# A fourth pair's q and k through the front's seven-product rounds, and P times V one tile a step

## The chip, the cores and the metric

One Trainium2 chip, and of it one core. The metric is the time of one execution on the device, in microseconds (us), by the median of several runs; the lower, the better.

## The reference

One layer of an encoder on x of 1024 rows (the sequence) by 1024 columns, in float32.

```python
h = rms_norm(x, g_pre_mix)
hc, bg, cg, q, k, v = jnp.split(h @ w_in, 6, axis=-1)          # six times 512 columns
y_conv = short_gated_conv(hc, bg, cg, w_conv)                  # bg * causal_conv3(cg * hc)
y_attn = chunked_band_attention(q, k, v, rel_bias)             # 8 heads of 64
y = jnp.concatenate([group_rms_norm(y_conv, g_conv_out, 8),
                     group_rms_norm(y_attn, g_attn_out, 8)], axis=-1) @ w_out
x = x + rms_norm(y, g_post_mix)
gate, up = jnp.split(rms_norm(x, g_pre_ffn) @ w_ffn_in, 2, axis=-1)
x = x + rms_norm((silu(gate) * up) @ w_ffn_out, g_post_ffn)    # 2816 hidden columns
```

In the attention a chunk of 64 queries sees its own chunk and the 8 before it: scores of q and k over 8, a learned bias by relative position, softmax, times v.

## The kernel before

Every engine has a hand-written program, and semaphores join them. Each float32 matrix product is made of three matmuls in fp32r: an operand is split into a high part (ScalarE) and a low part (VectorE), and high by high, high by low, low by high are summed in PSUM.

**The front.** Of the input projection, v is made first. Then come `FRONT` rounds of two 128-column chunks of `w_in` each. A round multiplies two by two blocks with seven block products in place of eight (`front_multiply`, L1171, twelve matmuls of 512 columns for a product). VectorE makes the sums of weights (`front_s`), the low parts (`front_low`) and the sums of products (`make_u2` to `make_c12`). Five rounds make the convolution's three inputs but for two chunks. The other `FRONT_PAIRS` rounds make q and k of one head pair each, the last pair first. All but the last round's q and k are stored in `query_scratch` (`store_qk`) and loaded again (`load_qk`) when the front's rows of the arena come free; pair 0's go directly into its operands. The loads of v and then of q, k are issued on SP's queue (L616, L653) once product 5 of the last round is done.

**The chunks that fill.** What the front does not make is made by `project`: `FILLED` chunks, 48 matmuls of 512 columns each, cut into eight pieces of six matmuls (`piece`, L934). They are the convolution's gate `cg` of the last group first and `bg` of it last, and between them q and k of the pairs that the front leaves out. `AHEAD` pieces run before attention. The table `FILLS` says how many run in each step of each pair. A finished half is drained from PSUM by ScalarE (q, k) or multiplied by VectorE (`cg`, `bg`).

**The attention.** Four head pairs `t`, each with nine steps `s`. A tile is 128 queries of both heads; tile `i` sees at most 640 keys (tiles 0 to 3 see 128 to 512). The parts of a tile:

- scores (L948), one PSUM area for each head; tiles 0 and 1 are scored together in step 0, tiles 2 and 3 in step 2, tiles 4 to 7 in their own steps. Scores of a tile wait for the biases of the one before (`biased`), since its area is the same.
- bias and row maximum on VectorE (`add_bias`, L2242), one instruction for each head and a small accumulator read behind it
- exponential on ScalarE (L1603)
- in the next step, transposes of P on TensorE (`transpose_p`, L958), four blocks for each head copied by ScalarE (`read_pT`, L1612) and, from tile 4 on, a fifth block (L966) copied by VectorE (`read_pT`, L2250)
- P times V (`times_v`, L976). Its result stands with head columns on the partitions, so it is copied by VectorE (`copy_o`, L2256), two tiles in one copy, transposed back by TensorE (`turn_back`, L984) and read by VectorE (`read_o`, L2261).

After a pair, ScalarE squares the outputs, VectorE sums the squares (L2366), GpSimd makes the factors (L773) and VectorE scales (`o_scale`, L2376). TensorE transposes the result (`transpose_o`, L1067), and VectorE multiplies it by the gain (`o_finish`, L2385). These four lie in steps 1 to 3 of the next pair. VectorE also makes the low parts of the next pair's q and k in step 7 (`low_q`, L2280, `low_k`, L2284) and, spread over the steps by `TAP_STEPS`, the last convolution's three taps.

Each engine takes its work strictly in the order written in its `step(t, s)`; nothing reorders it.

The out projection (L1219), the feed-forward products (L1334) and the last products (L1361) follow.

## Time and profile before

| | us |
|---|---|
| median of 3 runs | 1093.37 |
| lowest, highest | 1093.21, 1093.54 |
| the profiled execution | 1093.39 |
| its span | 1091.6 |
| TensorE busy | 1082.3 |
| VectorE busy | 795.6 |
| ScalarE busy | 473.5 |
| GpSimd busy | 150.9 |

The span is from the first to the last instruction on the core; the execution's own time has 1.8 us more around it. A row of a timeline has the start, the busy time, engine, line, operation, what it writes and reads, the shape and the number of instructions merged. Since TensorE's matmuls overlap in the pipeline, the time that a group takes from TensorE is read from its start to the start of the next row; the busy time in the row is some 0.1 us more. In brackets stands the idle time of the engine before the row, and what ended it.

The attention stretch runs from the first scores of pair 0 at 222.17 us to the end of pair 3's last transposes at 351.53.

### The profile page before, as it was taken

Reading aid. Unit: us, or ns where it says so; the run is one execution under the profiler, and the core shown is the slowest. Engines: PE = TensorE matmul, PEld = TensorE weight load, DVE = VectorE, ACT = ScalarE, POOL = GpSimd, SP = SyncE. Lnnn points to the kernel's source line nnn. Section 1 sums busy time; section 2 is a strip of 40 time slices with the busy share of each in tenths; the row PEclk is TensorE's granted clock in tenths of the full one; section 3 lists DMA queues with packets and bytes.
Section 4 is the critical chain, followed back from the end, with each engine's and each line's share of the span. In section 5 each row is a group of like instructions: output and inputs, shape, how many; then the busy total and the mean of one; then the engine's idle time right before and its main releaser. Section 6 shows DMA issues by size and latency. Waiting matters only on the chain.

```text
span 1091.6 us, 15835 instructions
## 1 busy us (share of the span) xinstructions
PE 1082.3 (99%) x5549; PEld 897.8 (82%) x5549; DVE 795.6 (73%) x1247; ACT 473.5 (43%) x802; POOL 150.9 (14%) x255
## 2 busy tenths in 40 slices
PE   8999999999999999999999999999999999999997
PEld 7888888878888888888888888888888888888886
DVE  6878888656767876968777878777787786555584
ACT  6642243356667665643232323323232256444541
POOL 2400000001101122102211211221121110000030
PEclk9999999999999999999999999999999999999999
DMA  7332123470010643517435543743554689777631
GB/s 270 107 126 77 43 58 127 160 251 2 21 59 20 231 158 114 172 50 249 139 118 188 173 154 116 221 140 119 183 175 151 210 322 363 232 232 231 212 115 77
DMA packets 117333, 168.28 MB, mean 154 GB/s; under 512 B 7880, under 2 KB 73432, under 8 KB 117280
## 3 DMA queue, kind: packets, MB, share of 16 engines
q1 hardware_dynamic: 99648, 107.50, 30.5%
q0 software_dynamic: 16464, 55.89, 14.7%
q10 hardware_dynamic: 1168, 4.20, 1.0%
q8 instruction: 32, 0.52, 0.2%
q14 instruction: 21, 0.17, 0.0%
HBM read 121.65 MB, written 49.04 MB: 156 GB/s over the span
## 4 chain that ended last, share of the span: by engine, by line
PE 95%; DVE 3%; DMA 1%; ACT 1%; issue 0%; POOL 0%; SPq 0%; DVEq 0%; POOLq 0%; ACTq 0%
PE psum L1334 35%; PE psum L1361 19%; PE psum L1171 11%; PE psum L934 8%; PE psum L1219 8%; PE psum L1083 4%; PE psum L976 3%; PE psum L948 2%; PE psum L958 2%; PE psum L923 1%; DMA arena<-in_x 1%; PE psum L1067 0%; PE psum L984 0%; PE psum L966 0%; PE psum L1180 0%
## 5 line engine op out<-in xcount | busy, mean ns | idle before, releaser
L1334 PE MATMUL psum<-arena_r,ws 128*128 128x512 f32 x960 | 224.1, 389 | 0.0
L1334 PEld LDWEIGHTS psum<-arena_r,ws 128*128 128x128 f32 x960 | 180.2, 188 | 37.4
L1334 PE MATMUL psum<-hT,ws 128*128 128x512 f32 x720 | 169.9, 389 | 0.0
L1334 PEld LDWEIGHTS psum<-hT,ws 128*128 128x128 f32 x720 | 135.1, 188 | 28.0
L1361 PE MATMUL psum<-hT 128*128 128x512 f32 (+1 forms) x600 | 135.2, 385 | 0.0
L1361 PEld LDWEIGHTS psum<-hT 128*128 128x128 f32 x600 | 111.3, 188 | 22.5
L2536 DVE TENSOR_TENSOR misc<-misc,psum 128x512 f32<-128x512 f32 x100 | 68.5, 685 | 48.3 <-PE psum L1334 46.1
L934 PE MATMUL psum<-hT,ws 128*128 128x512 f32 (+1 forms) x432 | 95.9, 373 | 0.0
L1171 PE MATMUL psum<-arena_r,ws 128*128 128x512 f32 x372 | 86.9, 389 | 0.0
L1814 ACT ACTIVATE ws<-o_raw 128x512 fp32r<-128x512 f32 x40 | 25.1, 628 | 138.5 <-DVE o_raw L2514 138.0
L934 PEld LDWEIGHTS psum<-hT,ws 128*128 128x128 f32 x432 | 72.5, 189 | 13.9 <-issue 2.2
L1171 PEld LDWEIGHTS psum<-arena_r,ws 128*128 128x128 f32 x372 | 69.8, 188 | 14.5
L1219 PE MATMUL psum<-ws,hT 128*128 128x512 f32 x348 | 81.2, 392 | 0.0
L1361 PE MATMUL psum<-ws 128*128 128x512 f32 (+1 forms) x348 | 78.1, 382 | 0.0
L1219 PEld LDWEIGHTS psum<-ws,hT 128*128 128x128 f32 x348 | 64.7, 188 | 13.3
L1361 PEld LDWEIGHTS psum<-ws 128*128 128x128 f32 x348 | 63.8, 188 | 12.6
L1171 PE MATMUL psum<-hT,ws 128*128 128x512 f32 x288 | 68.1, 390 | 0.0
L1814 ACT ACTIVATE ws<-raw 128x512 fp32r<-128x512 f32 x80 | 49.7, 623 | 40.3 <-PE psum L1334 39.3
L1171 PEld LDWEIGHTS psum<-hT,ws 128*128 128x128 f32 x288 | 53.9, 188 | 11.8 <-DVE ws L2044 0.7
L2531 DVE TENSOR_TENSOR ws<-raw,ws 128x512 fp32r<-128x512 f32 x80 | 55.2, 691 | 6.6
L2610 DVE TENSOR_TENSOR hT<-arena,hT 128x512 fp32r<-128x512 f32 x62 | 40.1, 688 | 20.0 <-ACT hT L1861 19.6
L1411 ACT ACTIVATE misc<-arena 128x1024 bf16<-128x1024 f32 (+2 forms) x37 | 34.8, 941 | 39.8 <-DVE arena L2662 16.6
(272 smaller groups left out, 1566.3 us busy)
## 6 DMA issues: line engine op xcount, KB each, us to landing
raw<-in_w_ffn_in SPq DMA_DIRECT2D x44, 512.0 KB, 4.4
act_scratch<-arena POOLq DMA_DIRECT2D x77, 256.0 KB, 3.2
raw<-in_w_in SPq DMA_DIRECT2D x22, 512.0 KB, 4.1
arena<-in_w_ffn_out POOLq DMA_DIRECT2D x22, 512.0 KB, 5.7
arena<-act_scratch SPq DMA_DIRECT2D x38, 256.0 KB, 3.5
arena<-in_x SPq DMA_DIRECT2D x16, 512.0 KB, 6.2
raw<-in_w_out SPq DMA_DIRECT2D x16, 512.0 KB, 3.4
raw<-act_scratch SPq DMA_DIRECT2D x26, 256.0 KB, 3.3
```

Source lines behind the costliest of these rows:

```text
L934: last = mm(PP[pair][:, at:end] if to is None else to, w[wp], hT[:, hp, k, at:end], start=(k == 0 and (wp, hp) == (0, 0)), stop=(k == KT - ...
L976: last = mm(PP[3][h * HD:(h + 1) * HD, at:at + P], v_tile(first + j, t * P + h * HD, HD), pT_of(t, tile_i)[:, h, j * P:(j + 1) * P], start ...
L1083: last = mm(v_bank(i), hT[:, hp, k, i * P:(i + 1) * P], v_weights(wp, k), start=(k == 0 and part == 0), stop=k == 7 and part == (1 if i < ...
L1171: last = mm(blocks(front_bank(n, i)), w[:, k * P:(k + 1) * P], b_operand(i, part, k), start=fresh_bank and k == 0 and w is hi and part == ...
L1219: last = mm(pair[:, half * 512:(half + 1) * 512], a, ws[:, slot, wp, half * 512:(half + 1) * 512], start=(first is not None and a is hi an ...
L1334: last = mm(blocks(bank), w[:, k * P:(k + 1) * P], b_operand(i, part, k), start=fresh_bank and k == 0 and w is hi and part == 0, stop=k == ...
L1361: last = mm(bank[:, at:end], a[:, n * P:(n + 1) * P], b[:, at:end], start=fresh_bank and a is ah and b is bh, stop=i == NP - 1 and a is al ...
L1411: go(dst, src, ACT.Square, scale=scale, accum_out=acc).then_inc(done[0], 1)
L1814: go(w_op(i)[0], w_raw[i], ACT.Copy).then_inc(w_hi, 1)
L2531: tt(lo, w_raw[i], hi.bitcast(F32), ALU.subtract).then_inc(w_split, 1)
L2536: tt(out, a, bank, ALU.add).then_inc(made, 1)
L2610: tt(lo, raw_ring[c % RING][:, part * 512:(part + 1) * 512], hi.bitcast(F32), ALU.subtract).then_inc(out_split, 1)
```

## The change

`FRONT_PAIRS` is 4: there are nine front rounds, and `FILLED` becomes 2, so that only `cg` and `bg` of the last group are left as filling chunks. 16 pieces stand in place of 32; `AHEAD` is 4 as before, and 12 run inside attention in place of 28. The splits of two chunks on ScalarE and VectorE go, and q and k of pair 3 are stored and loaded as those of pairs 1 and 2 are.

P times V is made one tile in each step, of the tile three steps back (V1 in step 4, V2 in step 5); tiles 6 and 7 go into steps 0 and 1 of the next pair. The turning back stays in pairs of tiles, one step later than before (steps 4, 6, 8, and step 1 of the next pair). VectorE copies an output pair behind the biases of steps 4, 6, 8 and reads it in the same step. In steps 4 and 6 a piece stands behind the turning back.

The transposes of a finished pair's outputs go from the banks beside the scores (`psum[:, 2560:3584]`) into the upper halves of the first four banks' pairs, which hold scores; they stand in step 1, ahead of the scores of tiles 2 and 3, and wait for the biases of tiles 0 and 1. Scores of tile 3 wait for VectorE's read of them, which is now two instructions of 512 columns.

What moves, at three places. TensorE, pair 0, from the scores of tile 4 (L948, one line later in the changed kernel) to those of tile 5, before and then changed:

```order
L948 MATMUL psum<-ws 128x384 [waits biased]
L948 MATMUL psum<-ws 128x384 x5
L948 MATMUL psum<-ws 128x256 x6
L958 MATMUL psum<-ident,arena 128x128 [waits pT_act,exp_done]
L958 MATMUL psum<-ident,arena 128x128 x7
L934 MATMUL psum<-hT,ws 128x512 [waits half_free1,w_split]
L934 MATMUL psum<-hT,ws 128x512 x5
L948 MATMUL psum<-ws 128x384 [waits biased]
```

```order
L949 MATMUL psum<-ws 128x384 [waits biased]
L949 MATMUL psum<-ws 128x384 x5
L949 MATMUL psum<-ws 128x256 x6
L974 MATMUL psum<-arena 64x128 [waits pT_act]
L974 MATMUL psum<-arena 64x128 x3
L959 MATMUL psum<-ident,arena 128x128 [waits pT_act,exp_done]
L959 MATMUL psum<-ident,arena 128x128 x7
L982 MATMUL psum<-ident,arena 128x128 [waits o_copied]
L982 MATMUL psum<-ident,arena 128x128
L935 MATMUL psum<-hT,ws 128x512 x6
L949 MATMUL psum<-ws 128x384 [waits biased]
```

Between the scores there stand now V1 and a turning back that waits for `o_copied`; the piece (L935) is behind it, where it followed T3.

TensorE, pair 0, from V4 in step 7 to T7 in step 8, before and then changed (L976 and L974 are P times V, L966 and L965 the fifth blocks):

```order
L976 MATMUL psum<-misc,arena 64x128 [waits tile_free,pT_dve,pT_act]
L976 MATMUL psum<-misc,arena 64x128 x9
L976 MATMUL psum<-arena 64x128 x10
L958 MATMUL psum<-ident,misc 128x128 [waits pT_act,exp_done]
L958 MATMUL psum<-ident,misc 128x128 x7
L984 MATMUL psum<-ident,arena 128x128 [waits o_copied]
L984 MATMUL psum<-ident,arena 128x128
L966 MATMUL psum<-ident,misc 128x128 x2
L934 MATMUL psum<-hT,ws 128x512 x6
L958 MATMUL psum<-ident,arena 128x128 [waits pT_act,exp_done]
```

```order
L974 MATMUL psum<-misc,arena 64x128 [waits pT_dve,tile_free,pT_act]
L974 MATMUL psum<-misc,arena 64x128 x9
L959 MATMUL psum<-ident,misc 128x128 [waits pT_act,exp_done]
L959 MATMUL psum<-ident,misc 128x128 x7
L965 MATMUL psum<-ident,misc 128x128 x2
L974 MATMUL psum<-arena 64x128 [waits pT_dve,pT_act]
L974 MATMUL psum<-arena 64x128 x9
L935 MATMUL psum<-hT,ws 128x512 x6
L959 MATMUL psum<-ident,arena 128x128 [waits pT_act,exp_done]
```

V5 left the side of V4, went behind T6 and got waits of its own (`pT_dve`); the turning back of step 7 went to step 8, and the piece stands behind V5.

VectorE, pair 1, steps 3 and 4, from behind the biases of tile 3, before and then changed:

```order
L2256 COPY arena<-psum 128x256 [waits o_psum]
L2085 TENSOR_SCALAR arena<-arena,params 128x1024
L2376 TENSOR_TENSOR arena<-o_raw,rst 128x1024 [waits o_rs,dve_seq]
L2240 MEMSET gate 128x1 [waits biased,scores_psum,o_ready]
L2242 ISA misc,nmax<-psum,arena 128x640
L2242 ISA nmax 128x1
L2240 MEMSET gate 128x1 [waits biased,scores_psum]
L2242 ISA misc,nmax<-psum,arena 128x640
L2242 ISA nmax 128x1
L2261 COPY o_raw<-psum 128x256 [waits o_back]
```

```order
L2373 TENSOR_TENSOR arena<-o_raw,rst 128x1024 [waits o_rs]
L2240 MEMSET gate 128x1 [waits biased,scores_psum,o_ready]
L2242 ISA misc,nmax<-psum,arena 128x640
L2242 ISA nmax 128x1
L2240 MEMSET gate 128x1 [waits biased,scores_psum]
L2242 ISA misc,nmax<-psum,arena 128x640
L2242 ISA nmax 128x1
L2256 COPY arena<-psum 128x256 [waits o_psum]
L2261 COPY o_raw<-psum 128x256 [waits o_back]
```

The copy of outputs 0 and 1 (waits `o_psum`) and the read after their turning back (`o_back`) both stand behind the biases of tile 4 now, and a tap left the place ahead of the scaling (waits `o_rs`). In step 3 of all pairs nothing else moved ahead of the scaling but the product with a gate half in pair 2.

The diff, cut to its core:

```diff
-    FRONT_PAIRS = 3
+    FRONT_PAIRS = 4
...
-        FILLS = [[1, 1, 1, 1, 1, 0, 1, 0, 1], [1, 1, 1, 1, 1, 0, 1, 0, 1], [1, 1, 1, 1, 1, 0, 1, 0, 1], [1, 2, 1, 1, 1, 0, 1, 0, 0]]
-        TAP_STEPS = (9, 11, 20)
+        FILLS = [[1, 0, 0, 1, 1, 0, 0, 0, 1], [0, 0, 0, 1, 1, 0, 0, 0, 1], [0, 0, 0, 1, 1, 0, 0, 0, 1], [0, 0, 0, 1, 1, 0, 0, 0, 0]]
+        TAP_STEPS = (5, 6, 10)
...
+        FILL_LAST = (4, 6)
...
-        OT_BANKS = psum[:, 2560:3584]
+        OT_BANKS = psum[:, 0:2048].rearrange("p (b h c) -> p h b c", h=2, c=512)[:, 1]
...
-                if i in (2, 4, 6):
-                    turn_back(t, i - 2)
-                elif n > 4:
-                    pe.wait_ge(tile_free, tile(t, i - 1) + 1)
+                if i in (3, 5, 7):
+                    turn_back(t, i - 3)
...
             def output(t, i):
 
-                copied(t, i + 1)
-                pe.wait_ge(tile_free, tile(t, i) + 1)
+                copied(t, i)
+                if i > 2:
+                    pe.wait_ge(pT_dve, t * 4 + min(i + 1, NT - 1) - 3)
+                if i % 2 == 0:
+                    pe.wait_ge(tile_free, tile(t, i) + 1)
                 times_v(t, i)
...
                     for i in scored(t, s):
+                        if i == 3 and t > 1:
+                            pe.wait_ge(oT_read, t - 1)
                         scores(t, i)
-                        if i == 2 and t > 1:
-                            pe.wait_ge(tile_free, tile(t - 1, NT - 2) + 2)
-                            transpose_o(t - 1, OT_BANKS)
                 if s == 0 and t == 0:
                     fill(t, s)
-                if s == 0 and t > 0:
-                    output(t - 1, NT - 2)
+                if s < 2 and t > 0:
+                    output(t - 1, NT - 2 + s)
                 if s == 0:
                     return
-                if s in (3, 5, 7):
-                    fill(t, s)
                 if s == 3 and t == 0:
                     pe.wait_ge(v_back, 64)
-                if s in (3, 5, 7):
+                if s > 2:
                     output(t, s - 3)
+                if s not in FILL_LAST:
+                    fill(t, s)
+                if s == 1 and t > 1:
+                    pe.wait_ge(biased, unit(t, 4))
+                    transpose_o(t - 1, OT_BANKS)
...
                 transpose_p(t, s - 1)
-                if s in (4, 6):
+                if s == 1 and t > 0:
+                    turn_back(t - 1, NT - 2)
+                if s in FILL_LAST:
                     fill(t, s)
...
                     add_bias(t, 2 * s)
                     add_bias(t, 2 * s + 1)
-                if s == 0 and t > 0:
+                if s == 1 and t > 0:
                     copy_o(t - 1, NT - 2)
-                if s in (3, 5, 7):
-                    copy_o(t, s - 3)
-                if s == 7 and more:
-                    low_q(t)
+                    if t > 1:
+                        o_finish(t - 1, OT_BANKS)
+                    read_o(t - 1, NT - 2)
+                if s in (4, 6, 8):
+                    copy_o(t, s - 4)
...
                 if s > 4:
                     read_pT(t, s - 1)
-                if s == 6:
+                if s in (4, 6, 8):
+                    read_o(t, s - 4)
+                if s == 6 or s == NT and more:
                     drain(t, s)
+                if s == 7 and more:
+                    low_q(t)
...
-                if s == 4:
-                    read_o(t, 0)
-                if s in (5, 7):
-                    read_o(t, s - 3)
...
+                if len(pair.shape) == 3:
+                    ts(row(t + PAIRS - 1, HALF), pair[:, 0, :], params[:, t - 1, 4:5], None, ALU.mult)
+                    ts(row(t + PAIRS - 1, HALF, HALF), pair[:, 1, :], params[:, t - 1, 4:5], None, ALU.mult).then_inc(oT_read, 1)
```

On ScalarE both exponentials of a tile stand ahead of the copy of the transposes in every step from 3 on; before, only in steps 3, 5, 7.

## Rows read from the trace of the kernel before

**Rows 1.** Page, part 1: busy us, share of the span, instructions of TensorE.

```profile
PE 1082.3 (99%) x5549; PEld 897.8 (82%) x5549; DVE 795.6 (73%) x1247; ACT 473.5 (43%) x802; POOL 150.9 (14%) x255
```

**Rows 2.** Windows by head pair: length, busy of PE, PEld, DVE, ACT, POOL; clock; DMA.

```profile
222.17:253.35 31.18, 31.11 (x267) 25.39 (x267) 19.55 (x64) 20.92 (x43) 0.83 (x2) 1.00 0.50 173
253.35:285.51 32.16, 32.16 (x305) 26.73 (x304) 23.37 (x69) 23.12 (x46) 3.39 (x1) 1.00 0.05 18
285.51:318.84 33.33, 33.33 (x312) 27.52 (x312) 22.88 (x68) 22.00 (x45) 2.91 (x1) 1.00 0.02 5
318.84:351.53 32.69, 32.69 (x313) 27.39 (x313) 21.81 (x67) 20.68 (x43) 2.90 (x1) 1.00 0.13 47
```

**Rows 3.** Timeline of PE, the front's last product and the first pieces.

```profile
213.91 2.88 PE L1171 MATMUL psum<-hT,ws 128*128 128x512 f32 x12
216.63 5.60 PE L934 MATMUL psum<-hT,ws 128*128 128x512 f32 x24
```

**Rows 4.** Timeline of PE, steps 4 to 8 of pair 1, then pair 2's first scores.

```profile
265.28 1.14 PE L948 MATMUL psum<-ws 64*128 64x384 f32 x12
...
271.59 1.09 PE L958 MATMUL psum<-ident,misc 128*128 128x128 f32 x8
272.52 0.38 PE L984 MATMUL psum<-ident,arena 128*128 128x128 f32 x2
272.74 0.38 PE L966 MATMUL psum<-ident,misc 128*128 128x128 f32 x2
273.05 1.15 PE L948 MATMUL psum<-ws 64*128 64x384 f32 x12
...
275.20 1.64 PE L934 MATMUL psum<-hT,ws 128*128 128x512 f32 x6
276.77 1.16 PE L948 MATMUL psum<-ws 64*128 64x384 f32 x12
...
279.00 1.26 PE L976 MATMUL psum<-arena 128*64 128x128 f32 x20
280.19 1.09 PE L958 MATMUL psum<-ident,misc 128*128 128x128 f32 x8
...
285.51 0.97 PE L948 MATMUL psum<-ws 64*128 64x256 f32 x12
286.41 1.31 PE L976 MATMUL psum<-misc,arena 128*64 128x128 f32 x20
```

**Rows 5.** Timeline of PE, pair 2, step 2: transposed outputs, then scores of tile 3.

```profile
291.48 1.09 PE L1067 MATMUL psum<-ident,arena 128*128 128x128 f32 x8
292.50 0.96 PE L948 MATMUL psum<-ws 64*128 64x512 f32 x6
```

**Rows 6.** Timeline of VectorE, pair 1, step 7: biases, copy, low part of q.

```profile
277.98 0.82 DVE L2242 CUSTOM_DVE_ANT_0 arena<-psum,arena 128x640 f32<-128x640 f32 x1 [0.42 <-issue]
...
279.73 0.08 DVE L2242 DVE_READ_ACCUMULATOR2_ANT nmax<- 128x1 f32 x1
280.38 0.42 DVE L2256 COPY arena<-psum 128x256 f32<-128x256 f32 x1 [0.56 <-PE psum L976]
280.72 1.22 DVE L2280 SCALAR_TENSOR_TENSOR ws<-arena,ws 128x1024 fp32r<-128x1024 f32 x1
```

**Rows 7.** Timeline of VectorE, pair 2, steps 2 to 4: transposed outputs, squares, bias, scaling.

```profile
292.82 1.28 DVE L2385 TENSOR_SCALAR arena<-psum,params 128x1024 f32<-128x1024 f32 x1
294.14 1.22 DVE L2366 TENSOR_REDUCE osq<-arena 128x16 f32<-128x1024 f32 x1
...
295.66 0.69 DVE L2242 CUSTOM_DVE_ANT_0 arena<-psum,arena 128x512 f32<-128x512 f32 x1
...
298.66 1.23 DVE L2376 TENSOR_TENSOR arena<-o_raw,rst 128x1024 f32<-128x1024 f32 x1 [0.43 <-POOL rst L773]
```

**Rows 8.** Timeline of GpSimd, pair 2: the factors.

```profile
295.71 2.91 POOL L773 TENSOR_TENSOR rst<-o_eps,mhalf 128x16 f32<-128x16 f32 x1 [30.14 <-DVE o_eps L2372]
```

**Rows 9.** Source line L616 (loads of v), the last of four, issued at 216.6.

```profile
DMA to landing us min/median/max: 11.3/11.7/12.1
```

More of the change, by code:

```diff
@@ L969, in times_v @@
             def times_v(t, i):
-                for tile_i in (i, i + 1):
-                    first, n = keys(2 * tile_i)
-                    at = OUT_AT + tile_i % 2 * P
-                    for j in range(n // P):
-                        for h in range(2):
-                            last = mm(PP[3][h * HD:(h + 1) * HD, at:at + P], v_tile(first + j, t * P + h * HD, HD),
-                                      pT_of(t, tile_i)[:, h, j * P:(j + 1) * P], start=(j == 0), stop=(j == n // P - 1))
-                last.then_inc(o_psum, 2)
+                first, n = keys(2 * i)
+                at = OUT_AT + i % 2 * P
+                for j in range(n // P):
+                    for h in range(2):
+                        last = mm(PP[3][h * HD:(h + 1) * HD, at:at + P], v_tile(first + j, t * P + h * HD, HD),
+                                  pT_of(t, i)[:, h, j * P:(j + 1) * P], start=(j == 0), stop=(j == n // P - 1))
+                last.then_inc(o_psum, 1)
             def turn_back(t, i):
@@ L1066, in transpose_o @@
                 for i in range(NT):
-                    last = tr(bank[:, i * P:(i + 1) * P], row(CR, P, i * P), ident[:, :])
+                    to = bank[:, i * P:(i + 1) * P] if len(bank.shape) == 2 else bank[:, i // 4, i % 4 * P:(i % 4 + 1) * P]
+                    last = tr(to, row(CR, P, i * P), ident[:, :])
                 last.then_inc(oT_psum, 1)
@@ L1674, in step @@
                     read_pT(t, s - 1)
-                if s < NT and s not in (3, 5, 7):
+                if s < 3:
                     exp(t, 2 * s + 1)
@@ L2298, in step @@
                     dve.wait_ge(qk_stored, 32 * (FRONT_PAIRS - 1))
-                if s == 0 or s == NT and more:
+                if s == 0:
                     drain(t, s)
```

17 lines of the change are left out of this document (4 added, 13 removed).

## The prediction

> **What bounds the kernel now.** The page's busy times come first: TensorE works 1082.3 of 1091.6 us [rows 1], so a change pays only if it takes work off TensorE without making it wait. Then the windows by pair over the attention stretch, 222.17 to 351.53 us: TensorE has 129.29 of 129.36 us, VectorE 87.62, ScalarE 86.73, granted clock 1.00 [rows 2] (the sums are those of the four rows). TensorE never waits there. What hides the chain from scores over bias and exponential to transposes and output is 28 pieces of filling. The timelines of TensorE and VectorE then tell what each item takes and how long the chain is once the pieces are gone [rows 4 to 9].
>
> I write S4 for the scores of tile 4, V4 for P times V, T4 for the transposes of P; a step's time is taken from the start of its scores.
>
> **The front round.** Twelve matmuls take 2.72 us, from 213.91 to 216.63 [rows 3], 227 ns each. A round is seven such groups, so one more costs 19.04 us, all of it on TensorE. Its VectorE and ScalarE work is of the kind the round before does beside full TensorE, so I take no wait for it; the extra store and load of q, k (4 more transfers, 2 MB) go through SP's queue behind the loads of v, and are wanted only at step 7 of pair 0. By the Trainium skill ("TensorE: Matmul & The Clock Gate", "Back-to-back issue gap") a sustained stream of 512-column matmuls needs about 131 ns each; the rows have 227 ns and decide; by the page the 12 matmuls that the change saves are worth 1.6 us, by the rows 2.7.
>
> **The pieces.** 16 pieces of 6 matmuls leave attention (28 there before, 12 after). One takes 1.57 us, from 275.20 to 276.77 [rows 4]: 25.1 us of TensorE time. Front and pieces together are 19.04 - 25.1 = -6.1 us if nothing else becomes late. Everything else turns on what does.
>
> **Steps 4 to 8.** VectorE's first bias starts 1.21 us after the scores (276.77 to 277.98), the pair of biases ends 1.83 later (279.73 + 0.08 - 277.98), a copy of 256 columns takes 0.42 [rows 4, 6]. For a semaphore between engines I take 0.05, an estimate. Turning an output back takes TensorE 0.22, a fifth block until the next scores 0.31, eight transposes 0.93, one V 1.19 (279.00 to 280.19) [rows 4].
> Step 4: TensorE comes to the turn back after S4, V1, T3, some 2.6 us. It waits for the copy of outputs, which VectorE now makes behind both biases: 1.21 + 1.83 + 0.42 + 0.05 = 3.5. Then turn 0.22 and the piece 1.57, which stands behind the turn: 5.3 until S5. The piece covers nothing.
> Step 5: S6 waits for both biases: 1.21 + 1.83 + 0.06 = 3.1.
> Step 6: as step 4 without a piece, with a fifth block: 3.5 + 0.22 + 0.31 = 4.0.
> Step 7: V5 now waits for VectorE's read of tile 6's fifth block, which follows both biases and the block itself: T6 ends at 3.2 (276.77 to 279.00 for S7 and V4, then 0.93), 0.4 to the copy's start (an estimate), the copy 0.42: about 4.05 where TensorE is there at 3.4.
> Step 8: V5 1.19, piece 1.57, T7 0.93, turn 0.22, fifth 0.31: 4.2, TensorE's own.
> Sum 20.6 us a pair, where before the same steps take 20.2 with four pieces (S4 of pair 1 at 265.28, S0 of pair 2 at 285.51 [rows 4]). In pair 3 step 8 has no piece but the turned outputs (1.02 [rows 5]), and VectorE puts two splits (1.22 [rows 6] and about 0.5) ahead of the read that V5 waits for: 20.6 - 1.57 + 1.02 + 1.1 = 21.15.
>
> **Steps 0 to 3.** S0 and S1 take 0.90 (285.51 to 286.41), V6 and V7 some 2.34 [rows 4]: V7 ends at 3.24.
> Pair 3: the turned outputs 1.02 to 4.26; VectorE reads them 0.19 later, in two halves now, 1.28 [rows 7] plus about 0.07 for the split; then it reads the turned output (0.34, what a copy of 0.42 takes in a row of them, 280.38 to 280.72 [rows 6]), biases 4 and 5 about 1.4 (estimate between the wider pairs), and sums the squares. That sum starts at 7.5. It takes 1.22, the small add 0.2, biases 6 and 7 about 1.6 (twice 0.69 and the gaps that also part the wider ones) [rows 7]: S4 at 10.6.
> Pair 2: the same, but the last tap (1.28, by the 1024-column rows) stands in VectorE's queue between biases 0, 1 and 2, 3, and the turned outputs wait for all four: S4 at 11.6.
> Pair 1: no turned outputs; copy of output 6 behind biases 2, 3, turn back, then S2 at 4.3: S4 at 9.7. The second tap, in step 5, adds about 0.4 to step 6.
> Pair 0: the first V waits for v. Its last load landed 12.1 us after its issue at 216.6 [rows 9], 6.5 us after S0 (222.17 [rows 2]). With one piece in place of four ahead of it, V0 is due at 4.9 (TensorE's terms, and S2 waits 0.3 for biases 2, 3). So V0 at 6.6, then V0 and T2 about 1.0, piece 1.57: S4 at 9.1. Left uncovered on that path are 1.7 us.
>
> **The root on GpSimd.** Scaling the outputs stands on VectorE behind the factors that GpSimd makes: from the sum of squares' start at 294.14 to the scaling at 298.66 are 4.52 us, of which GpSimd works 2.91 [rows 7, 8]. It is queued ahead of bias 8. Now biases 6 and 7 end 3.05 after the sum's start, S4 follows at 3.1, and VectorE would be due for bias 8 at 4.3; the scaling runs from 4.5 to 5.75 (1.23 [rows 7]). Bias 8, and with it the turn in step 4, is late by 1.45 us in pairs 1 to 3. (In pair 2 the product with the gate, 0.68, fits into VectorE's wait.)
>
> **The sum.** Pair 0: 9.1 + 20.6 = 29.7. Pair 1: 9.7 + 1.45 + 0.4 + 20.6 = 32.15. Pair 2: 11.6 + 1.45 + 20.6 = 33.65. Pair 3: 10.6 + 1.45 + 21.15 = 33.2. Together 128.7 us where 129.36 stood [rows 2]: 16 pieces go, and attention takes as long as before. Behind pair 3 I take no change: the order there is the same. So -0.7 + 19.04 = +18.3: span 1109.9 us, and with the 1.8 us around it in the profiled execution (1093.39 against 1091.6; the median of the runs is 1093.37, the same) 1111.7 us.
>
> **Rivals.** First, TensorE stays the bound, which ends faster: 1093.4 - 6.1 = 1087.3 us. For it: after the change it still has 104 us of work in attention, VectorE about 85 [rows 2], so the means leave room. Against it: the engines run in order, and in step 4 the copy is ready at 3.5 us, TensorE at 2.6; it decides for this rival only if a pair of biases and the copy took a microsecond less, and 1.83 us is plain in the rows. Chance 0.08.
> Second, the chain holds but its extras don't: v lands in time (1.7), the root's 1.45 three times is hidden, V5 isn't held up (0.65 three times, 1.1 + 0.65 in pair 3): 10 us less, 1102 us. For it, GpSimd's spans are rough, and the time of landing depends on what shares the DMA engines. Chance 0.15.
> Third, TensorE's clock. The granted clock is 1.00, the level of 2.4 GHz, in all four rows while TensorE has no gap [rows 2]; after the change it idles a fifth of that time. At 1.2 instead of 2.4 GHz its terms on the path double: 1.79 in step 4, 0.53 in step 6, 4.2 in step 8, 6.5 us a pair, 26 us if it lasts through all four, 1138 us; nothing in the trace shows it. Chance 0.06. The Trainium skill ("TensorE: Matmul & The Clock Gate", "Part 4: PE-mode transpose") says that transposes don't count as work for the clock as matmuls do, which speaks against a stage with fewer matmuls and the same transposes; no row here shows a clock below 1.00.
> That the change doesn't do what it says has no room: the order shows nine rounds and 12 pieces.
>
> **How the numbers follow.** The forecast has 0.71. Its errors are those of thirty hops and of three estimated biases: 5 us down, 4 up, 1107 to 1116. The range reaches down to the second rival: 1101 to 1116; the first and third, 0.14, stay outside. A measurement tells this kernel from no change beyond about 0.2%, 2.2 us. Faster: the first rival and a little of the second, 0.09; within: 0.03; slower: 0.88.
>
> **What would show it.** In the profile after: seven groups of 2.72 us more in the front; four S0-to-S0 distances near 30, 32, 34 and 33 us; TensorE idle some 20 to 25 us in attention, before the turn back (released by VectorE's copy of outputs), before scores (by the biases) and before V5 (by the fifth block's read); VectorE waiting for GpSimd's factors in pairs 1 to 3. I am wrong if S4 to S5 takes under 4.5 us, if TensorE's idle time in attention is under 10 us, or if the front grows by other than 19.

## The result, and the profile after

The changed kernel takes 1112.1 us (median of 4 runs, 1110.4 to 1113.1) where the kernel before takes 1093.4: a ratio of 1.017, with a 95% interval of 1.0152 to 1.0187. It is slower by 18.7 us; 1111.7 was forecast. In the profiled execution the span is 1110.2 us against 1091.6.

The page of the kernel after, part 1 (busy us, share of the span, instructions):

```profile
PE 1085.1 (98%) x5537; PEld 897.7 (81%) x5537; DVE 804.5 (72%) x1263; ACT 475.9 (43%) x805; POOL 149.9 (13%) x255
```

TensorE has 12 matmuls fewer than before [rows 1] and is busy for 2.8 us more. The front round's 19.0 us more and the pieces' 25.1 less would have given 6.1 less, so some 9 us of "busy" is time in which the same matmuls took longer. Where the time went is told by the windows. Those of the kernel after, with the columns of [rows 2]: the four head pairs, from the first scores of one to the first scores of the next, and then all that follows attention.

```profile
241.00:269.74 28.74, 26.75 (x245) 21.29 (x244) 17.03 (x59) 19.79 (x42) 0.83 (x2) 1.00 0.52 201
269.74:301.97 32.23, 28.04 (x279) 22.56 (x278) 22.97 (x69) 21.44 (x44) 2.93 (x1) 1.00 0.01 2
301.97:335.68 33.71, 29.07 (x287) 23.29 (x286) 23.55 (x70) 21.46 (x44) 2.91 (x1) 1.00 0.03 7
335.68:370.14 34.46, 29.73 (x290) 24.02 (x289) 21.83 (x69) 21.59 (x45) 2.90 (x1) 0.95 0.15 57
370.14:1110.20 740.06, 734.05 (x3373) 611.18 (x3371) 536.40 (x760) 294.33 (x488) 119.54 (x211) 1.00 0.54 179
```

Attention starts at 241.00 where it started at 222.17: the front has grown by 18.83 us, seven groups of twelve matmuls. The four pairs take 129.14 us in place of 129.36, although 96 matmuls of 512 columns (25.1 us) have left them. What follows takes 740.06; of before it was 740.07 (1091.60 - 351.53). So the whole difference is the front round, and the question is why attention gave nothing back.

The waits of TensorE in the kernel after, from 241 to 370.14 us (what waited, for what; us in total, times, longest):

```profile
PE psum L982 <- DVE arena L2256: 8.3, 8, 2.3
PE psum L974 <- DVE misc L2250: 3.9, 5, 1.5
PE psum L949 <- DVE nmax L2242: 1.4, 3, 0.5
PE psum L949 <- DVE arena L2384: 0.7, 2, 0.3
PE psum L1067 <- DVE nmax L2242: 0.7, 1, 0.7
PE psum L974 <- DMA arena<-value_scratch: 0.3, 1, 0.3
```

TensorE had none of these before [rows 2]. The largest is the turning back (L982), which waits for VectorE's copy of outputs (L2256). Then come P times V (L974), which waits for VectorE's read of the transposes (L2250), and the scores (L949), which wait for biases.

Steps 4 to 8 of pair 1 in the kernel after, on TensorE. These rows answer to [rows 4]. The first is the scores of tile 4, the last the first scores of pair 2.

```profile
279.36 1.14 PE L949 MATMUL psum<-ws 64*128 64x384 f32 x12 [0.43 <-DVE nmax L2242]
280.43 0.66 PE L974 MATMUL psum<-arena 128*64 128x128 f32 x8
281.02 1.09 PE L959 MATMUL psum<-ident,arena 128*128 128x128 f32 x8
284.26 0.44 PE L982 MATMUL psum<-ident,arena 128*128 128x128 f32 x2 [2.15 <-DVE arena L2256]
284.46 1.64 PE L935 MATMUL psum<-hT,ws 128*128 128x512 f32 x6
286.03 1.16 PE L949 MATMUL psum<-ws 64*128 64x384 f32 x12
...
291.00 1.09 PE L974 MATMUL psum<-arena 128*64 128x128 f32 x16 [0.60 <-DVE misc L2250]
...
297.83 1.31 PE L974 MATMUL psum<-arena 128*64 128x128 f32 x20 [0.61 <-DVE misc L2250]
299.07 1.66 PE L935 MATMUL psum<-hT,ws 128*128 128x512 f32 x6
...
301.97 0.97 PE L949 MATMUL psum<-ws 64*128 64x256 f32 x12
```

In step 4 TensorE has scores, one V and eight transposes behind it and then stands still for 2.15 us. The piece of filling (284.46) is the next thing in its queue, but it stands behind the turning back, so it can't fill the gap. What TensorE waits for is seen on VectorE, in the same step of the kernel after:

```profile
280.77 1.23 DVE L2373 TENSOR_TENSOR arena<-o_raw,rst 128x1024 f32<-128x1024 f32 x1 [1.47 <-POOL rst L774]
282.04 0.82 DVE L2242 CUSTOM_DVE_ANT_0 misc<-psum,arena 128x640 f32<-128x640 f32 x1
...
283.04 0.82 DVE L2242 CUSTOM_DVE_ANT_0 misc<-psum,arena 128x640 f32<-128x640 f32 x1
...
283.79 0.42 DVE L2256 COPY arena<-psum 128x256 f32<-128x256 f32 x1
```

VectorE waits 1.47 us for GpSimd's factors (`rst`), scales the outputs for 1.23, and only then adds the two biases and copies. The first bias starts 2.68 us after the scores (279.36 to 282.04), where without this it starts after 1.21 [rows 4, 6]: 1.47 us late, forecast 1.45.

### The profile page after: what moved, and what is told of

Its sections match the earlier page's. It is cut to its first block, busy times and chain, and to the rows that moved or that the text cites. A ratio compares the mean times of both kernels' runs of the same rounds, so it can differ in the third digit from the quotient of the medians.

```text
span 1110.2 us, 15869 instructions
## 1 busy us (share of the span) xinstructions
PE 1085.1 (98%) x5537; PEld 897.7 (81%) x5537; DVE 804.5 (72%) x1263; ACT 475.9 (43%) x805; POOL 149.9 (13%) x255
## 3 DMA queue, kind: packets, MB, share of 16 engines
q1 hardware_dynamic: 100224, 109.59, 30.7%
## 4 chain that ended last, share of the span: by engine, by line
PE 66%; DVE 1%; issue 1%; POOL 0%; ACT 0%; DVEq 0%; POOLq 0%
PE psum L1334 34%; PE psum L1361 18%; PE psum L1219 8%; PE psum L935 4%; PE psum L924 1%; PE psum L974 0%; POOL rst L774 0%; PE psum L1067 0%; DVE arena L2242 0%; PE psum L982 0%; DVE arena L2728 0%; ACT misc L1411 0%; DVE osq L2363 0%; DVE ws L1939 0%; DVE arena L2668 0%
## 5 line engine op out<-in xcount | busy, mean ns | idle before, releaser
L1334 PE MATMUL psum<-arena_r,ws 128*128 128x512 f32 x960 | 224.1, 389 | 0.0
L1334 PEld LDWEIGHTS psum<-arena_r,ws 128*128 128x128 f32 x960 | 180.2, 188 | 37.4
L1334 PE MATMUL psum<-hT,ws 128*128 128x512 f32 x720 | 169.9, 389 | 0.0
L1334 PEld LDWEIGHTS psum<-hT,ws 128*128 128x128 f32 x720 | 135.1, 188 | 28.0
L1171 PE MATMUL psum<-arena_r,ws 128*128 128x512 f32 x420 | 98.1, 389 | 0.0
L1171 PEld LDWEIGHTS psum<-arena_r,ws 128*128 128x128 f32 x420 | 78.8, 188 | 16.4
L1814 ACT ACTIVATE ws<-o_raw 128x512 fp32r<-128x512 f32 x40 | 25.1, 629 | 139.0 <-DVE o_raw L2515 138.5
L1171 PE MATMUL psum<-hT,ws 128*128 128x512 f32 x324 | 76.6, 390 | 0.0
L935 PE MATMUL psum<-hT,ws 128*128 128x512 f32 (+1 forms) x336 | 71.6, 368 | 0.0
L1171 PEld LDWEIGHTS psum<-hT,ws 128*128 128x128 f32 x324 | 60.7, 188 | 13.2 <-DVE ws L2044 0.7
L935 PEld LDWEIGHTS psum<-hT,ws 128*128 128x128 f32 x336 | 56.4, 192 | 10.4 <-issue 1.4
```

The source lines that it names most:

```text
L935: last = mm(PP[pair][:, at:end] if to is None else to, w[wp], hT[:, hp, k, at:end], start=(k == 0 and (wp, hp) == (0, 0)), stop=(k == KT - ...
L1171: last = mm(blocks(front_bank(n, i)), w[:, k * P:(k + 1) * P], b_operand(i, part, k), start=fresh_bank and k == 0 and w is hi and part == ...
L1334: last = mm(blocks(bank), w[:, k * P:(k + 1) * P], b_operand(i, part, k), start=fresh_bank and k == 0 and w is hi and part == 0, stop=k == ...
L1814: go(w_op(i)[0], w_raw[i], ACT.Copy).then_inc(w_hi, 1)
```

## The experiments

Each kernel was timed against the kernel before on the same chip. Steps and letters are those of the prediction. For a quick view, here is where the pairs begin in each kernel's profile, as lengths in us. Start is the first scores of pair 0, and pair 3 ends 740.06 us before the end of the span, as in the two kernels above (within 0.05 in the others).

| kernel | start | pair 0 | pair 1 | pair 2 | pair 3 | sum |
|---|---|---|---|---|---|---|
| before | 222.17 | 31.18 | 32.16 | 33.33 | 32.69 | 129.4 |
| after | 241.00 | 28.74 | 32.23 | 33.71 | 34.46 | 129.1 |
| E1 scaling later | 241.30 | 28.78 | 30.75 | 32.22 | 31.5 | 123.2 |
| E2 piece first | 240.92 | 28.93 | 30.83 | 32.29 | 31.6 | 123.6 |
| E3 front alone | 241.34 | 26.43 | 29.32 | 32.07 | 30.1 | 117.9 |
| E4 order alone | 221.96 | 34.23 | 35.76 | 37.26 | 37.9 | 145.2 |
| E5 pieces elsewhere | 238.37 | 28.92 | 30.64 | 32.83 | 30.6 | 123.0 |
| E6 E5, scaling later | 238.73 | 29.33 | 30.77 | 32.70 | 30.5 | 123.3 |
| E7 three mends | 241.43 | 27.26 | 29.24 | 30.75 | 30.7 | 117.9 |
| E8 thin pieces | 241.25 | 26.33 | 33.37 | 32.14 | 32.3 | 124.1 |
| E9 E3 mended | 241.25 | 26.45 | 29.53 | 30.80 | 30.2 | 117.0 |
| E10 E7 and tap | 241.24 | 27.90 | 29.20 | 31.00 | 30.6 | 118.7 |

### E1: the scaling behind the copy of outputs

The theory says that in step 4 the turning back is late by VectorE's biases and copy, and that GpSimd's root with the scaling behind it puts 1.45 us on top in pairs 1 to 3. E1 takes the scaling out of the way and leaves the rest.

```diff
 (VectorE, step s of pair t)
+                if s == 4 and t > 0:
+                    o_scale(t)          # behind the biases and the copy of step 4
-                if s == 3 and t > 0:
-                    o_scale(t)
```

> The changed kernel, with the scaling of the outputs moved on VectorE from the end of step 3 to step 4, behind biases 8, 9 and the copy of outputs 0, 1. Nothing else. Theory (VectorE's queue and GpSimd's factors set the wait of the turn back in step 4): the wait of 2.2 us before that turn back in pairs 1 to 3 falls to the 0.7 of pair 0, 4.4 us less, 1107.6 us; and the fall of TensorE's clock after the longest of these waits in pair 3 (some 1.3 us) should go too, 1106.4. Rival (TensorE is held by the pair of biases alone, the scaling is hidden): within 1 us of 1112.

Measured: 1106.3 us (1105.8 to 1106.4), ratio 1.0117 (1.01 to 1.0133), 5.8 less than the changed kernel. Step 4 of pair 1 on TensorE in E1:

```profile
279.70 1.15 PE L949 MATMUL psum<-ws 64*128 64x384 f32 x12 [0.44 <-DVE nmax L2242]
...
283.12 0.44 PE L982 MATMUL psum<-ident,arena 128*128 128x128 f32 x2 [0.67 <-DVE arena L2256]
283.32 1.64 PE L935 MATMUL psum<-hT,ws 128*128 128x512 f32 x6
```

The wait of 2.15 is now 0.67: 1.48 less. From scores 4 to the turning back are 3.42 us (279.70 to 283.12), where 3.5 was forecast without the root. Pairs 1 and 2 are each shorter by 1.5; pair 3 by 3.0, of which half belongs to the clock (below). GpSimd's root is shown as a cost of this order.

### E2: the piece of step 4 ahead of the turning back

The same wait, seen from the other side: the piece stays in step 4, but TensorE does it while VectorE is busy.

```diff
 (TensorE, transposes of tile i and what follows; i == 3 is step 4)
+                if i == 3:
+                    fill(t, 4)
                 if i in (3, 5, 7):
                     turn_back(t, i - 3)
...
-                if s in FILL_LAST:
+                if s in FILL_LAST and s != 4:
                     fill(t, s)
```

> The changed kernel, with the piece of step 4 put ahead of the turning back instead of behind it. Theory (the turn back is reached before its copy, and the piece behind it covers nothing): the piece fills the wait, 0.7 us less in pair 0 and 1.57 us less in pairs 1 to 3, 5.4 us in all, and 1.3 us more if the clock no longer falls in pair 3: 1105.4 to 1106.7 us. Rival (the chain of scores, biases and scores holds the steps, and a wait that is filled comes back before the next scores): under 1 us less.

Measured: 1106.0 us (1105.4 to 1107.2), ratio 1.0116 (1.0099 to 1.0133), 6.1 less. In E2:

```profile
281.99 1.63 PE L935 MATMUL psum<-hT,ws 128*128 128x512 f32 x6
284.38 0.44 PE L984 MATMUL psum<-ident,arena 128*128 128x128 f32 x2 [0.75 <-DVE arena L2258]
```

The turning back comes as late as in the changed kernel (4.9 us after scores 4 in both: 279.36 to 284.26 there, 279.47 to 284.38 here), but 1.57 us of work now lies inside the wait. That the piece "covers nothing" where the change puts it is shown. The work is the same to the instruction; its place in one queue is worth 1.4 us in pairs 1 and 2 each and 2.9 in pair 3, where the clock's fall goes, too.

### E3 and E4: the front round alone, the order alone

The change has two parts that can be had singly: nine front rounds with 12 pieces, and the new order of V, copies and turned outputs. E3 is the kernel before with the first, E4 the changed kernel without it.

```diff
 (E3, against the kernel before; E4 is the same lines the other way, against the changed one)
-    FRONT_PAIRS = 3
+    FRONT_PAIRS = 4
-        FILLS = [[1, 1, 1, 1, 1, 0, 1, 0, 1], [1, 1, 1, 1, 1, 0, 1, 0, 1], [1, 1, 1, 1, 1, 0, 1, 0, 1], [1, 2, 1, 1, 1, 0, 1, 0, 0]]
-        TAP_STEPS = (9, 11, 20)
+        FILLS = [[1, 0, 0, 1, 1, 0, 0, 0, 1], [0, 0, 0, 1, 1, 0, 0, 0, 1], [0, 0, 0, 1, 1, 0, 0, 0, 1], [0, 0, 0, 1, 1, 0, 0, 0, 0]]
+        TAP_STEPS = (5, 6, 10)
```

> The kernel before with nine front rounds and 12 pieces placed as the change has them, but with P times V, copies, turns and transposed outputs in the order of before. Theory (part of the loss is the new order's: turn backs behind the copy in steps 4 and 6, V5 behind the fifth block): steps 4 to 8 take some 18.5 us in place of 20.6, steps 1 to 3 still wait for the factors; 8 us less than the changed kernel, 1104 us, slower than before by 1%. Rival A (the loss is all in taking pieces away): 1110 to 1112. Rival B (the loss is all in the order): 1087, which is before less 6.1 us.

> The changed kernel with eight front rounds and the 28 pieces inside attention of before, so that only the order of P times V, copies, turns and transposed outputs is changed. Theory: the waits before the turns in steps 4 and 6 (0.9 and 0.3) and before V5 (0.6) stay, four times each, the wait for the factors goes since two more pieces stand in steps 1 and 2: 7 us more than before, 1100 us. Rival A (the order costs nothing while pieces are there): 1093 to 1094. Rival B (all the loss is the order's): 1110 or more.

Measured: E3 1101.0 us (1100.9 to 1102.5), ratio 1.0074 (1.0057 to 1.009). E4 1109.2 us (1109.0 to 1109.4), ratio 1.0145 (1.0128 to 1.0162). The first is 3 us under what was expected, the second 9 over it: both miss.

The two together make a square. With the old order the front round and its 12 pieces cost 7.5 us, with the new one 2.9. With 28 pieces the new order costs 15.8, with 12 it costs 11.1. So each part slows the kernel by itself, and the order by more. In E3 attention is 11.5 us shorter than before (117.9 against 129.4), although 25.1 us of pieces have left it: 9.5 us are waits, most of them of scores for biases (rows under E5), and the front takes 19.2 us more. That 28 pieces would hide most of the order's waits, as was expected of E4, is wrong. The windows of E4, pairs 0 to 3:

```profile
221.96:256.19 34.23, 32.15 (x267) 25.54 (x266) 19.73 (x64) 21.45 (x43) 0.82 (x2) 1.00 0.45 156
256.19:291.95 35.76, 33.29 (x303) 26.86 (x302) 23.52 (x69) 23.31 (x46) 2.93 (x1) 1.00 0.05 16
291.95:329.21 37.26, 34.39 (x311) 27.63 (x310) 23.09 (x69) 22.65 (x45) 2.91 (x1) 1.00 0.07 21
329.21:367.15 37.94, 33.76 (x314) 27.52 (x313) 21.80 (x67) 21.20 (x44) 2.90 (x1) 1.00 0.10 37
```

TensorE is busy for 133.59 of 145.19 us there. It idles for 11.6 where it idled for 0.07 before, and its matmuls, the same as before, take 4.3 us more. The expectation had counted 7 us of waits and nothing for longer matmuls. It also took VectorE's wait for the factors to be gone; it is still there, 0.70, 1.41 and 1.50 us in pairs 1 to 3, and the turning back of step 4 waits 1.30, 1.35 and 1.75 us in them against 0.80 in pair 0. Idle time and longer matmuls both show in rows of E4, pair 1:

```profile
271.57 0.44 PE L982 MATMUL psum<-ident,arena 128*128 128x128 f32 x2 [1.30 <-DVE arena L2256]
271.77 1.64 PE L935 MATMUL psum<-hT,ws 128*128 128x512 f32 x6
...
278.17 1.09 PE L974 MATMUL psum<-arena 128*64 128x128 f32 x16 [0.57 <-DVE misc L2250]
...
283.25 1.31 PE L974 MATMUL psum<-misc,arena 128*64 128x128 f32 x20
284.50 1.09 PE L959 MATMUL psum<-ident,misc 128*128 128x128 f32 x8
...
286.42 1.31 PE L974 MATMUL psum<-arena 128*64 128x128 f32 x20 [0.61 <-DVE misc L2250]
287.66 1.66 PE L935 MATMUL psum<-hT,ws 128*128 128x512 f32 x6
```

Again each piece stands right behind the instruction that waits (271.77 behind 271.57, 287.66 behind 286.42). And a V that has no other V behind it takes 1.25 us to the next group (283.25 to 284.50, 286.42 to 287.66 is 1.24), where two in a row took 1.14 (277.86 to 279.00) and 1.19 [rows 4]. The first of the two in the kernel before:

```profile
277.86 1.31 PE L976 MATMUL psum<-misc,arena 128*64 128x128 f32 x20
```

### E5 and E6: where the pieces stand in the old order

If the place of a piece decides, the old order with nine rounds should do better with pieces where E3 waits. The waits of TensorE in E3, through its four pairs:

```profile
PE psum L948 <- DVE nmax L2242: 5.8, 10, 1.6
PE psum L984 <- DVE arena L2256: 2.2, 4, 0.6
PE psum L958 <- DVE arena L2385: 1.5, 2, 0.8
```

E5 brings pieces into steps 1, 2 and 6, two of them from ahead of attention and the rest from steps 3 and 8; E6 is E5 with the scaling in step 4.

```diff
 (E5, against E3)
-        AHEAD = 4
-        FILLS = [[1, 0, 0, 1, 1, 0, 0, 0, 1], [0, 0, 0, 1, 1, 0, 0, 0, 1], [0, 0, 0, 1, 1, 0, 0, 0, 1], [0, 0, 0, 1, 1, 0, 0, 0, 0]]
-        TAP_STEPS = (5, 6, 10)
+        AHEAD = 2
+        FILLS = [[1, 0, 1, 1, 1, 0, 1, 0, 0], [0, 1, 0, 0, 1, 0, 1, 0, 0], [0, 1, 1, 0, 1, 0, 0, 0, 0], [0, 1, 1, 0, 1, 0, 0, 0, 0]]
+        TAP_STEPS = (3, 4, 7)
 (E6, against E5)
+                    if t > 0:
+                        o_scale(t)      # in step 4
-                if s == 3 and t > 0:
-                    o_scale(t)
```

> Nine front rounds and the order of before, as in the run that measured 1101.0 us, with the pieces put where TensorE waited in that run: two of the four pieces ahead of attention go inside it (14 inside), and they stand in steps 1, 2, 4 and 6 (before the turn back of outputs 6, 7, before T1, before S5 and S7) instead of 3 and 8; the taps go to steps 4, 5 and 8 of pair 1. Theory (a piece costs its 1.57 us only where TensorE doesn't wait; the order of before with well placed pieces gives most of the 6.1 us): waits of 0.6 to 0.9 before turn backs, 0.8 before T1, 0.7 before S7 and 1.6 behind the last tap are filled, 8 us less, 1093 us. Rival (the biases set the pace, so that a filled wait comes back at the next scores): 1099 to 1101.

> The same kernel as the one above, with the scaling of the outputs on VectorE in step 4, behind biases 8 and 9, instead of step 3. Theory (bias 8 waits for the factors of GpSimd, 0.75 us in each of pairs 1 to 3, and S5 with it): up to 2 us less than the one above, 1091 to 1092, which would be under the kernel before. Rival: the piece in step 4 hides it already, no change.

Measured: E5 1103.5 us (1103.1 to 1104.3), ratio 1.0095 (1.0078 to 1.0112), E6 1103.6 (1103.2 to 1103.9), ratio 1.0092 (1.0075 to 1.0109). E5 misses, and is 2.5 us slower than E3; E6 takes what E5 takes, as its rival said. The waits of TensorE in E5:

```profile
PE psum L958 <- ACT misc L1612: 3.3, 3, 1.2
PE psum L984 <- DVE arena L2256: 2.5, 2, 1.4
PE psum L976 <- ACT arena L1612: 2.5, 3, 1.1
PE psum L948 <- DVE nmax L2242: 2.3, 5, 0.7
```

The scores' waits went from 5.8 to 2.3 us, as meant. But the places that gave their pieces up now wait for ScalarE: the transposes of step 8 for an exponential (3.3), P times V of step 3 for the copy of the transposes (2.5). The turning backs of step 4 in pairs 1 and 2, which had a piece of step 3 ahead of them, wait for their copy (2.5). These waits were not in E3, or were small, because its pieces lay over them. In all TensorE waits 11.0 us where it waited 9.5 in E3: with 14 pieces and more places that need one, moving pieces moves the wait. In E6 the scores' waits fall further, to 1.4 us, but the reads of turned outputs now stand behind the scaling, and P times V waits for them in pairs 1 to 3, 0.6 us together: the wait has moved again, and the whole gains nothing.

### E7 and E10: the waits of the new order mended

E7 puts E1 and E2 together and puts the piece of step 8 ahead of V5, too. E10 is E7 with the last tap moved from the end of step 0 of pair 2 into step 8 of pair 1.

```diff
 (E7, beside the edits of E1 and E2)
+                if s == 8:
+                    fill(t, s)
...
-                if s not in FILL_LAST:
+                if s not in FILL_LAST and s != 8:
                     fill(t, s)
 (E10, against E7)
-        TAP_STEPS = (5, 6, 10)
+        TAP_STEPS = (5, 6, 9)
```

> The changed kernel with three mends together: the scaling in step 4, the piece of step 4 ahead of the turn back, and the piece of step 8 ahead of V5. Theory (each wait has a cause of its own, so the mends add where they don't fill the same wait): the scaling gives the 5.8 us measured alone, the piece of step 4 then finds 0.7 us to fill in each pair, 2.7, and the piece of step 8 0.6 in pairs 0 to 2, 1.8: 1101.8 us. Rival (one chain holds the whole, so that the second mend finds nothing): 1105 to 1106.

> The changed kernel with its three mends (1101.1 us) and the last tap in step 8 of pair 1 instead of step 0 of pair 2. Theory (the tap between the biases holds up the transposed outputs, 0.7 us before them in the changed kernel): 0.7 to 1.3 less, 1100.1 us, and no version of the new order comes near the 1093.4 us of the kernel before. Rival: no change, since in step 8 the tap delays the read of tile 7's fifth block instead.

Measured: E7 1101.1 us (1100.7 to 1102.0), ratio 1.0072 (1.0055 to 1.0089): 11.0 us less than the changed kernel, by nothing but places in two queues, and within 0.7 of what was expected. It is also what E3 takes (1101.0): with these three places mended, the new order no longer costs more than the old. E10 1101.4 (1101.2 to 1101.8), ratio 1.0072 (1.0055 to 1.0089): no gain. In E10 the turned outputs of pair 2 still wait for the biases, and VectorE has the tap ahead of them:

```profile
299.12 1.27 DVE L2091 SCALAR_TENSOR_TENSOR arena<-arena,params 128x1022 f32<-128x1022 f32 x1
...
302.69 1.09 PE L1071 MATMUL psum<-ident,arena 128*128 128x128 f32 x8 [0.94 <-DVE nmax L2246]
```

The move took the tap from between the four biases to ahead of all four. The turned outputs wait for the last of them, so they still have the tap ahead of them: the first bias starts 2.30 us after the pair's first scores (298.34 to 300.64) where it starts after 0.99 in E7. E10 can't tell, then, whether the tap holds the turned outputs up. Its rival named the right outcome for another reason; the read of tile 7's fifth block stands ahead of the tap and is not delayed. The changed kernel itself tells more. Its turned outputs start 4.09 us after the pair's first scores in pair 2, behind a wait of 0.68, and 3.35 after them in pair 3 (335.68 to 339.03), which has no tap and no wait:

```profile
306.06 1.09 PE L1067 MATMUL psum<-ident,arena 128*128 128x128 f32 x8 [0.68 <-DVE nmax L2242]
...
339.03 1.10 PE L1067 MATMUL psum<-ident,arena 128*128 128x128 f32 x8
```

The prediction put pair 2's 1.5 us over pair 1 down in part to the tap. The size was right (33.71 - 32.23 = 1.5), and by this comparison the tap is worth 0.7 us of it, where the forecast had 1.0. No run has the new order without a tap ahead of those biases.

### E8: how much of the time is the pieces' own

The twelve pieces inside attention work on 64 columns instead of 512. This leaves out seven eighths of the columns of these products, so the output isn't the reference's.

```diff
+                    n = HALF if q < AHEAD else 64
-                    last = project(g % 2, k, 3, ((half * HALF, (half + 1) * HALF),), half == 1, half_bank())
+                    last = project(g % 2, k, 3, ((half * HALF, half * HALF + n),), half == 1, half_bank()[:, 0:n])
```

> The changed kernel, with the matmuls of the 12 pieces inside attention 64 columns wide instead of 512: seven eighths of these products are left out, which makes them 1.3 us shorter each, 15.7 us of TensorE's time in all. Theory (TensorE isn't the bound in steps 1 to 3 and 5, but the pieces behind the turn back of step 4 and behind V5 lie on the path): 5.2 us from step 4, 2.4 from step 8 (then ScalarE's copy of the transposes is late), 1.3 from pair 0: 9 us less, 1103 us. Rival A (TensorE's work is the bound throughout): 15.7 less, 1096.4. Rival B (VectorE alone is the bound): 1110 to 1112.

Measured: 1107.2 us (1107.1 to 1111.0), ratio 1.0138 (1.0119 to 1.0156), 4.9 less than the changed kernel and not 9. Two things were off. A thin piece takes 0.76 us in place of 1.57, so it is 0.81 shorter and not 1.3, and TensorE's clock fell twice, in pair 1 (steps 4 and 5) and in pair 3 (step 4). In pair 3 the granted clock was 0.51 from 343.70 to 345.60 and 1.00 again from 347.20. The window of the fall in pair 1:

```profile
282.20:289.30 7.10, 7.10 (x43) 6.26 (x43) 4.03 (x9) 3.44 (x8) 0.00 (x0) 0.52 0.00 0
```

Pair 1 is 1.1 us longer than in the changed kernel, for its clock. Pairs 0 and 2, where the clock kept 1.00, can be compared, and they answer the question. In pair 2 the scores of tile 4 come 11.38 us after the first scores (11.39 in the changed kernel), so the piece of step 3 cost nothing: with it thin, TensorE waits 0.63 us for ScalarE's exponential instead. Step 4 takes 5.99 us in place of 6.79 and steps 7 and 8 take 7.63 in place of 8.38. The pieces behind the turning back and behind V5 thus lie on the path with all that they take, as the prediction had it; pair 0 gives 0.8 us in each of these two places, too.

### E9: the old order with the tap and the scaling moved

```diff
 (against E3)
-        TAP_STEPS = (5, 6, 10)
+        TAP_STEPS = (5, 6, 9)
+                    if t > 0:
+                        o_scale(t)      # in step 4
-                if s == 3 and t > 0:
-                    o_scale(t)
```

> The run with nine front rounds and the order of before (1101.0 us), all pieces where they are there, with the last tap in step 8 of pair 1 instead of step 0 of pair 2, and the scaling behind biases 8 and 9. Theory (the 1.6 us wait before pair 2's scores of tile 2 is the tap's, 1.3 of it; bias 8 waits 0.75 us for the factors in pairs 1 to 3, of which S5 shows 0.3 each): 1101.0 - 1.3 - 0.9 = 1098.8 us. Rival (both are hidden by the next wait): 1101.

Measured: 1100.0 us (1100.0 to 1100.4), ratio 1.0061 (1.0044 to 1.0077), half way between the two expectations and the fastest kernel with nine front rounds. The table splits the two edits: pair 2, which had the tap, is shorter by 1.3, and pairs 1 and 3, where only the scaling moved, are longer by 0.2 and 0.1. In E3 the scores of tile 2 in pair 2 waited 1.61 us for the biases behind the tap; in E9 they wait 0.31:

```profile
302.16 0.79 PE L948 MATMUL psum<-ws 64*128 64x384 f32 x6 [0.31 <-DVE nmax L2242]
```

The same move of the tap gave nothing in E10, and VectorE's rows show why. Before its copy of outputs in step 0 of pair 2 it idles for 1.92 us in E3 (the copy starts at 300.58). The tap, moved ahead of this idle time, fills it: in E9 0.74 are left (copy at 300.71). About 1 us of the 7.5 that E3 loses is thus the place of the tap.

In the new order the copy stands in step 1, and VectorE has no such idle time ahead of the four biases. The scaling, worth 1.5 us a pair in the new order, gives nothing in the old one. There the copy of outputs stands ahead of the scaling, so that the turning back doesn't wait for it; the scores of tile 5 no longer wait (0.30, 0.29 and 0.20 us in E3), but P times V right behind them waits for the read of turned outputs (0.20, 0.30 and 0.18).

No version here beats the kernel before.

## Why the prediction was right, point by point

- **What bounds the kernel.** Right in what it says of the changed kernel: TensorE, which had no wait, has 20, and 19 of them are for VectorE. That 28 pieces are what hides the chain is only half of it: E4 has all of them and waits 11.5 us.
- **The front round.** 18.83 us measured, 19.04 forecast; and no wait in it. The rows decided: the twelve matmuls of a group still take 2.72 us, 227 ns each. The 131 ns of the Trainium skill ("TensorE: Matmul & The Clock Gate", "Back-to-back issue gap") don't hold for these matmuls.
- **Steps 4 to 8.** In pair 1, scores 4 to the next pair's first scores take 22.61 us (279.36 to 301.97); 20.6 + 1.45 + 0.4 = 22.45 was forecast. Single steps: 6.67 (forecast 6.75 with the root), 3.22 (3.1), 4.34 (4.0 + 0.4 for the tap), 4.24 (4.05), 4.14 (4.2). The mechanism of the longest, that VectorE makes the copy behind both biases and that the piece behind the turning back covers nothing, is shown by E1 and E2 singly, and E8's pairs 0 and 2 show the second half of it again.
- **The root on GpSimd.** 1.47 measured by the bias's start, 1.45 forecast, and E1 gives 1.5 a pair back.
- **Steps 0 to 3.** Pairs 1, 2 and 3: 9.6, 11.4 and 10.65 us measured, 9.7, 11.6 and 10.6 forecast. (The 0.19 us from the turned outputs to VectorE's read stand in no row; [rows 5, 7] have 0.25 from end to start, and the changed kernel 0.20.) Pair 0: 8.0 and not 9.1. The step that failed there is v's landing: the first V starts 5.4 us after the first scores, where 6.5 was taken from the DMA row [rows 9]. The last load was issued 6.4 us ahead of the first scores (234.6) and landed after 11.7, where the forecast took 5.6 us and 12.1. The first V starts after 6.5 us in E2 and 6.2 in E10, so the term varies from run to run by a microsecond.
- **Pair 3.** 34.46 us measured, 33.2 forecast. Step 4 takes 8.12 us (346.33 to 354.45) where 6.75 was forecast and pairs 1 and 2 take 6.67 and 6.79. The 1.4 us are the clock (last section), which stood among the rivals and not in the sum. So the total's nearness owes something to luck: two errors of opposite sign, -1.0 in pair 0 and +1.3 in pair 3.
- **The idle time.** 20 to 25 us of idle TensorE were forecast. The windows show 129.14 - 113.59 = 15.6. The step that failed is that time lost was taken for idle time. Without the 16 pieces TensorE would be busy for 129.29 - 25.1 = 104.2 us; it is busy for 113.6, with the same matmuls. 15.6 idle and 9.4 in longer matmuls make 25.0, which is what was meant. Some 1.3 of the 9.4 are the piece at the lower clock (2.91 us busy against 1.64). A group ahead of a wait also counts as busy to its own end: eight transposes 1.09 us, where they take 0.93 to the next group if one follows at once (the ends are modelled, so the split between the two is rough; the sum isn't).
- **The rivals.** The first (TensorE stays the bound) is wrong; TensorE waits 20 times. The second (the extras are hidden) is wrong for the root and V5, and right by 1.1 us for v. The third (the clock) came true for one stretch of 3 us, 1.4 us in place of 26.
- **What the prediction did not do** is to part the order from the pieces. Its sum is right, but it reads as if taking pieces away had cost the gain. E3 and E4 show that pieces and front round cost 7.5 us by themselves and the order 11.1 on top, and that the order would have cost 15.8 with all pieces in. The expectations of E4 and E5 missed for reasons of this kind: E4's took the wait for the factors to be covered by pieces that stand ahead of other instructions, and E5's counted the waits that its pieces would fill and not those that they had been filling.

What stays open: how the rest of the 9.4 us of longer matmuls divides into lone V's and groups in front of waits; and what an order would look like that has the pieces of E3 in exactly its ten waiting places, with the places of E5 covered too. It was not tried.

## What to carry to other kernels

Filling work on an engine that takes its instructions in order hides only a wait that stands behind it in that queue; before counting how much filling there is, find for each wait the piece ahead of it (E2 moved one piece in each pair by one place, for 6 us). When an operation is put behind others on a helper engine "since there is time", look at what the main engine asks for next: a copy of 0.42 us behind two biases, and behind another engine's root, made TensorE wait 2.15 to 2.26 us for the turning back in each of three pairs. And when two changes come as one, time them as a square of four kernels: here each part's cost depends by 4.7 us on the other.

## What the runs showed of the hardware

**The clock can fall in a kernel that is 98% busy.** Windows of the kernel after in pair 3, step 4 and the piece behind it, and the two rows of TensorE's timeline where it changes:

```profile
346.33:351.20 4.87, 2.77 (x28) 2.22 (x28) 3.25 (x8) 2.70 (x6) 1.41 (x1) 0.99 0.00 0
351.20:354.45 3.25, 3.18 (x10) 2.15 (x10) 0.44 (x2) 1.54 (x3) 0.00 (x0) 0.50 0.03 5
```

```profile
351.27 0.69 PE L982 MATMUL psum<-ident,arena 128*128 128x128 f32 x2 [2.17 <-DVE arena L2256]
351.61 2.91 PE L935 MATMUL psum<-hT,ws 128*128 128x512 f32 x6
```

After one V, eight transposes and a wait of 2.17 us the granted clock is 0.50, the level of 1.2 GHz, and the piece of 1.57 us takes 2.84 (351.61 to 354.45); then it is back at 2.4 GHz. The same step of pairs 1 and 2, with waits of 2.15 and 2.26, kept 1.00, so such a wait is not enough by itself. In E8, where pieces are thin, a fall came in pair 1 after a wait of 2.14 and lasted 7.1 us, with TensorE busy all through it. A second one came in pair 3 at 343.7, where the waits ahead of it were only 0.64 and 0.49, around six transposes and behind a thin piece; it lasted some 3.4 us, into the transposes of step 4. So the fall doesn't need a wait of 2 us. E4 kept 1.00 through a wait of 1.75. In E1 and E2, whose longest wait in step 4 is 0.9, every window of attention has 1.00. By the Trainium skill ("TensorE: Matmul & The Clock Gate", "Part 4: PE-mode transpose") transposes don't count as work for the clock; that transposes and waits stood ahead of each fall agrees with it, though the same steps of other pairs had both and kept 1.00, and no run here has the one without the other. The changed kernel's four runs lie 2.7 us apart and E8's 3.9, where the kernel before stays within 0.4: a fall that comes in one execution and not in another would do that. The mean granted clock on record for each execution agrees in E8, 0.991 in the one of 1111.0 us against 0.994 to 0.996 in the three of 1107.1 to 1107.2; in the changed kernel it is 0.997 in the longest and 0.998 in the others, too small a difference to show it.

**GpSimd's work of 2.9 us on the factors** kept its length in all pairs (2.93, 2.91, 2.90), and the 1.47 us that VectorE waits for it in pair 1 are what E1 takes off TensorE's wait there (2.15 to 0.67).
